# Head rounds of a two-layer transformer block: order of logarithms, weight splits, decay rows and panels

## The chip, the cores and the metric

One core of a Trainium2 chip runs the whole program as one launch. The metric is device time in microseconds (us), median over runs. The engines are TensorE (PE in the profile; its weight loads are PEld), VectorE (DVE), ScalarE (ACT), GpSimd (POOL) and SyncE (SP), which issues most transfers. An engine works through its own instructions in the order in which they are written; between engines the order is set by semaphores.

## The reference, cut to what matters

Two layers over 256 latent and 256 context tokens of width 1024, all float32. Each layer has a feed-forward half, a token mixer and a second feed-forward half. The mixer has three branches (attention, short convolution, gated delta rule); the change is in the third.

```python
DN_HEADS, DN_DIM, CONV_WIDTH = 8, 128, 3
def _dn_inputs(p, dn_conv):
    y = jax.nn.silu(_dwconv(p[6], dn_conv)).astype(jnp.float32)
    q, k, v = [t.reshape(B, T, DN_HEADS, DN_DIM) for t in jnp.split(y, 3, axis=-1)]
    return (_l2norm(q), _l2norm(k), v) + tuple(...)
def _gated_delta_chunked(q, k, v, g, beta, s0):
    gc = jnp.cumsum(chunks(g), axis=-1)
    diff = gc[..., :, None] - gc[..., None, :]
    decay_mat = jnp.where(incl, jnp.exp(jnp.where(incl, diff, 0.0)), 0.0)
    a_mat = jnp.where(strict, jnp.einsum('nbhid,nbhjd->nbhij', kb, kc) * decay_mat, 0.0)
    sol = lax.linalg.triangular_solve(a_mat, rhs, left_side=True, lower=True, unit_diagonal=True)
    attn_intra = jnp.einsum('nbhid,nbhjd->nbhij', qc, kc) * decay_mat
    def step(s, inp): ...   # v_new = u - w s; o = q e^g s + attn_intra v_new; s = s e^g_last + k' v_new
```

It runs in both directions of time for eight heads in each layer. In the last layer only the 256 latent tokens need an output, so queries and output gates are wanted for those alone; keys and values for all 512.

## The kernel before

Every weight matrix comes from HBM as panels of 128x1024 floats. SP loads a panel into `raw`; ACT rounds it to `whi` and DVE subtracts to `wlo` (both called `split`). PE then multiplies 24 times (8 tiles of rows, each `whi` by `uh`, `whi` by `ul`, `wlo` by `uh`), 512 tokens wide or 256. Four panels make a block, and panel j of a block goes to PSUM bank j. SP loads a panel when the `wlo` of the one in its place a block earlier is written; ACT rounds when PE is done with it (`panel_done`).

**A head round.** `heads` on each engine runs the delta rule. One head's four panels (query, key, value, gate) are one block B. Round b works on two heads at once: for head b-1 it solves the triangular system and runs the recurrence, in both directions d = 0 and 1; for head b it makes the inputs. Rounds 1 to 7 of each layer are of this form (`follow`), 14 in all; rounds 1 to 6 are a hardware loop. Round 8 finishes the last head. On PE a round is:

- 14 half levels (`level(v, d)`), in which the inverse of the triangle is doubled. DVE masks one product into `Pm`, ACT copies the other to `QTh`; PE waits for both two half levels later. After each, `project(3)` issues three of the panel multiplications.
- three products that correct the inverse: `lx_sum`, `x2_sum`, `xf_sum`, each followed by `project(3)`. ACT copies the result of the second (L891 in the profile); DVE makes `XTf` from the third (L1668).
- four steps s of the recurrence: `ks_sum`, DVE's `Rr` (L1675), `y_sum`, DVE's `vd`, `ds_sum`, DVE's new state `St` (L1692, L1695), with 15 panel multiplications between them.
- the front of the next head (`output_and_front`): transposes of value and key, the Gram matrix, 27 panel multiplications, and DVE's `Gs`, `AT` (`low_a`), a split and `first_level`.

A round issues 96 panel multiplications: panels 2 and 3 of block B, then 0 and 1 of B+1. Panel 0 of B+1 begins at the third correction, at `project(3)` behind `xf_sum`. It writes bank 0. In the same round bank 0 holds the squared sum of the key, so `project` waits there for `pair_done[0]`, which ACT raises when it has taken the logarithms (`prep_rsqrt`, L785 to L789).

Each half level leaves DVE and ACT room for other work, and their part of `head` puts it at hand-picked places `at` = 2v + d: the convolution of the three inputs (`prep_in`, `prep_tap`, `prep_conv`, `prep_silu`), the splits, and on DVE the decay rows (`decay`): per direction four `scalar_tensor_tensor` of 128x128, `gcr` minus the column `hgc` plus a mask. `gcr` is a row of cumulated gates that a transfer broadcasts (`load_rows`). ACT makes the exponential of a whole row of 512 (`decays`, L806). POOL multiplies `Qt` and `IT` at the head of a round (L489, L493) and subtracts the low half of the output (L495).

Of the kernel before, what the change touches and what calls it, by code (L numbers as in the profile page):

```python
# [134 lines left out]
def build(nc, stream, h_in, vecs_in, rows_in, wab_in, consts_in, cond_in, gcd, out):  # L135
# [7 lines left out]
    with ctx:  # L143
# [329 lines left out]
        def _(pool):  # L473
# [7 lines left out]
            def heads(l):  # L481

                c0 = CTX if l == DEPTH - 1 else 0
                with pool.Fori(0, DNH) as b:
# [9 lines left out]
                    pool.wait_ge(E["bh_ready"], o + 1)  # L494
                    pool.tensor_tensor(bl[:, ds(b, 1), c0:T].rearrange("p a t -> p (a t)"), gate[:, c0:T],  # L495
                                       bh[:, ds(b, 1), c0:T].rearrange("p a t -> p (a t)").bitcast(f32),
                                       ALU.subtract).then_inc(E["head_ready"], 1)
# [11 lines left out]
        def _(act):  # L509
# [219 lines left out]
            def prep_in(l, b, n):  # L729
# [6 lines left out]
                act.activation(pre[:, j, a:2, 1:257], bank[j][:, :].rearrange("p (s t) -> p s t", s=2)[:, a:2, :], ACT.Identity,  # L736
# [43 lines left out]
            def prep_rsqrt(l, b):  # L780
# [8 lines left out]
                act.sem_inc(pair_done[0], 1)  # L789
                for n, a in ((0, 0), (1, c0)):  # L790
                    act.activation(hrs[:, n, a:T], hrs[:, n, a:T], ACT.Exp, scale=-0.5).then_inc(E["l2_rstd"], 1)
# [8 lines left out]
            def decays(l, b):  # L800
# [39 lines left out]
            def head(l, b, follow):  # L840
# [7 lines left out]
                for v in range(7):  # L848
                    for d in range(2):
# [15 lines left out]
                        if at == 4:  # L865
                            split(B, 3)
# [9 lines left out]
                        if at == 8:  # L876
                            split(B + 1, 0)
# [5 lines left out]
                        if at == 11:  # L883
                            split(B + 1, 1)
                        if at == 12:
# [11 lines left out]
                log_exp()  # L897
                if follow:
                    prep_rsqrt(l, b)
                    decays(l, b)  # L900
                    gate_in(l, b)
                output_and_front(l, b, True, follow)

            def heads(l):
# [27 lines left out]
                split(B0 + 1, 2)  # L932
                with steps.loop(1, DNH - 1, 3) as b:
# [255 lines left out]
        def _(dve):  # L1189
# [345 lines left out]

            def prep_conv(l, b, n):
# [27 lines left out]
            def decay(l, b, d):  # L1564

                f = l * DNH + b
                if d == 0:
                    wait(dve, E["dm_ready"], 2 * f)
                    dve.tensor_copy(hgc[:, :], tab[:, ds(b, 1), 8 * HB_GC:8 * HB_GC + 8].rearrange("p a n -> p (a n)")).then_inc(E["hgc_ready"], 1)
                    dve.wait_ge(E["hgc_ready"], f + 1)  # L1570
                    dve.wait_ge(gcr_loaded, 16 * f + 16)
                    wait(dve, E["it_ready"], 2 * f)
                for c in range(TC):
                    last = stt(out=DT[:, d, 128 * c:128 * c + 128], in0=gcr[:, d, 128 * c:128 * c + 128],
                               scalar=hgc[:, 4 * d + c:4 * d + c + 1], in1=cst[:, C_NM + 128 * d:C_NM + 128 * d + 128],
                               op0=ALU.subtract, op1=ALU.add)
                last.then_inc(E["dm_ready"], 1)

            def output_and_front(l, b, output, front):
# [20 lines left out]
                if front:  # L1600
# [4 lines left out]
                    if not output and l == 0:  # L1605
                        decay(l, b, 0)
                    q_norm(l, b)
                    if not output:
                        for d in range(0 if l else 1, 2):
                            decay(l, b, d)  # L1610
                if front:
# [6 lines left out]
                    if output:  # L1618
                        split(P[("head", l)][0] + b + 1, 2)
# [11 lines left out]
            def head(l, b, follow):  # L1631
                B = P[("head", l)][0] + b
                o = l * DNH + b - 1
                if follow:
                    prep_vec(l, b)
                for v in range(1, 7):
# [1173 lines left out]
```

## Time and profile before

| | |
|---|---|
| median of 3 runs | 3138.06 us (3137.23 to 3140.63) |
| profiled execution, its time | 3135.32 us |
| its span, first to last instruction | 3133.5 us |
| TensorE busy | 3026.1 us, 97% of the span |
| mean granted clock of TensorE | 0.992 of full speed |
| follow rounds in layer 0 | about 53.9 or 52.4 us each |
| follow rounds in layer 1 | about 48.9 to 49.8 us each |

A line of the profile names the line of the kernel, engine, operation and tiles (`out<-in`). "Idle before" is how long the engine had nothing to run before that instruction, with what released it. PEclk and granted clock are shares of TensorE's full 2.4 GHz. Rounds are told apart by POOL's instruction L495, one in each.

### The profile page before, as it was taken

To read this page: it belongs to the slowest core of one execution; us is meant where nothing else is said; L and a number is where in the kernel's file an instruction comes from. 1 tells how busy PE (TensorE), PEld (TensorE's weight loads), DVE (VectorE), ACT (ScalarE), POOL (GpSimd) and SP (SyncE) were. 2 spreads that over 40 slices of the span, in tenths; PEclk is the share of its full clock that TensorE was granted. 3 is DMA by queue.
4 is the path that set the end of the run, shared out by engine and by line. 5 is a ranking of instruction groups with operands and counts; after the bars stand their busy time and mean duration, and the time that the engine had idled before them with its cause. 6 is when DMAs were issued, how large, how long until landed. Compare 5 with 4: busy or idle time off the path is not lost.

```text
span 3133.5 us, 49986 instructions
## 1 busy us (share of the span) xinstructions
PE 3026.1 (97%) x17660; PEld 2506.2 (80%) x17660; DVE 2050.5 (65%) x3838; ACT 1408.8 (45%) x2222; POOL 135.9 (4%) x120
## 2 busy tenths in 40 slices
PE   7999999999999999999999999999989999899998
PEld 5888877777787678888888888888777779699887
DVE  4776777777634744445665775757777776766777
ACT  4222365665544642234222342224665566654654
POOL 0000010101000000001000100001000000000000
PEclk9999999999999999999999999999999999999999
DMA  7544421111122022233443533533111114145554
GB/s 272 188 174 174 167 70 47 47 54 47 55 94 74 28 81 95 100 101 103 174 161 136 187 134 136 197 137 127 62 60 51 50 61 142 61 141 175 165 185 153
DMA packets 101843, 365.61 MB, mean 117 GB/s; under 512 B 11216, under 2 KB 12880, under 8 KB 101584
## 3 DMA queue, kind: packets, MB, share of 16 engines
q1 hardware_dynamic: 98384, 353.02, 32.9%
q10 hardware_dynamic: 3328, 10.81, 1.0%
q8 instruction: 86, 1.41, 0.2%
q14 instruction: 45, 0.37, 0.0%
HBM read 362.67 MB, written 1.11 MB: 116 GB/s over the span
## 4 chain that ended last, share of the span: by engine, by line
PE 85%; ACT 6%; DVE 5%; issue 3%; DMA 1%; ACTq 0%; DVEq 0%; SPq 0%; POOLq 0%; POOL 0%
PE bank L2003 65%; PE bank L1982 4%; PE bank L1984 2%; PE bank L2334 1%; PE bank L2274 1%; DVE wlo L1198 1%; ACT whi L519 1%; PE bank L2342 1%; PE bank L2276 1%; PE bank L2540 1%; PE bank L2354 1%; PE bank L2513 1%; PE bank L2352 1%; PE bank L2324 1%; ACT gc_row L1051 1%
## 5 line engine op out<-in xcount | busy, mean ns | idle before, releaser
L2003 PE MATMUL bank<-uh,whi 128*128 128x512 f32 (+1 forms) x2688 | 1019.9, 379 | 36.5 <-ACTq L789 25.3
L519 ACT ACTIVATE whi<-raw 128x1024 fp32r<-128x1024 f32 x520 | 548.3, 1056 | 996.1 <-PE bank L2003 968.7
L2003 PE MATMUL bank<-uh,wlo 128*128 128x512 f32 (+1 forms) x2688 | 977.2, 364 | 0.3 <-DVE scr L1685 0.3
L2003 PE MATMUL bank<-ul,whi 128*128 128x512 f32 (+1 forms) x2688 | 977.4, 364 | 0.0
L1198 DVE TENSOR_TENSOR wlo<-raw,whi 128x1024 fp32r<-128x1024 f32 x520 | 637.1, 1226 | 386.6 <-ACT whi L519 377.6
L2003 PEld LDWEIGHTS bank<-uh,whi 128*128 128x128 f32 x2688 | 510.4, 190 | 132.2 <-issue 50.8
L2003 PEld LDWEIGHTS bank<-uh,wlo 128*128 128x128 f32 x2688 | 509.4, 190 | 78.5 <-issue 6.2
L2003 PEld LDWEIGHTS bank<-ul,whi 128*128 128x128 f32 x2688 | 510.9, 190 | 69.3 <-issue 6.3
L2003 PE MATMUL bank<-bh,whi 128*128 128x512 f32 (+1 forms) x930 | 340.1, 366 | 0.8 <-DVE bl L1920 0.8
L2003 PE MATMUL bank<-bl,whi 128*128 128x512 f32 (+1 forms) x930 | 337.6, 363 | 0.0
L2003 PE MATMUL bank<-bh,wlo 128*128 128x512 f32 (+1 forms) x930 | 337.6, 363 | 0.0
L2003 PEld LDWEIGHTS bank<-bh,whi 128*128 128x128 f32 x930 | 175.4, 189 | 29.3 <-DVE bl L1920 1.0
L2003 PEld LDWEIGHTS bank<-bl,whi 128*128 128x128 f32 x930 | 175.5, 189 | 28.3 <-issue 0.7
L2003 PEld LDWEIGHTS bank<-bh,wlo 128*128 128x128 f32 x930 | 175.5, 189 | 27.3
L1217 DVE SCALAR_TENSOR_TENSOR scr<-ada_raw,gc_row 128x1024 f32<-128x1024 f32 x128 | 156.2, 1220 | 0.0
L1217 DVE SCALAR_TENSOR_TENSOR xtf<-ada_raw,lmat 128x1024 f32<-128x1024 f32 x128 | 155.9, 1218 | 0.0
L1982 PE MATMUL bank<-uh,whi 128*128 128x512 f32 x416 | 144.0, 398 | 1.4 <-DVE uh L1299 0.9
L479 POOL TENSOR_TENSOR scr<-scr 128x512 f32<-128x512 f32 (+1 forms) x36 | 51.6, 1432 | 2159.3 <-ACT scr L556 2159.3
L1640 DVE TENSOR_TENSOR ada_raw<-bank,cst 128x512 f16<-128x512 f32 x192 | 128.1, 686 | 22.3 <-PE bank L2276 21.9
L852 ACT ACTIVATE ada_raw<-bank 128x512 f16<-128x512 f32 x192 | 111.9, 587 | 18.7 <-PE bank L2276 16.9
L1438 DVE TENSOR_TENSOR scr<-scr,bank 128x512 f32<-128x512 f32 x66 | 45.4, 688 | 114.4 <-PE bank L2003 112.6
L2274 PEld LDWEIGHTS bank<-ada_raw 128*128 128x128 f16 x896 | 51.3, 98 | 84.3 <-issue 49.4
(304 smaller groups left out, 3746.4 us busy)
## 6 DMA issues: line engine op xcount, KB each, us to landing
raw<-stream SPq DMA_DIRECT2D x524, 512.0 KB, 3.3
ada_raw<-stream SPq DMA_DIRECT2D x131, 512.0 KB, 4.3
gc_row<-gc_rows ACTq DMA_DIRECT2D x16, 512.0 KB, 3.6
h<-h_in SPq DMA_DIRECT2D x1, 2048.0 KB, 10.3
m<-stream SPq DMA_DIRECT2D x4, 512.0 KB, 12.2
cst<-consts SPq DMA_DIRECT2D x1, 1104.0 KB, 12.6
scr<-stream SPq DMA_DIRECT2D x2, 512.0 KB, 17.1
lmat<-cond ACTq DMA_DIRECT2D x2, 512.0 KB, 4.0
```

The source lines that it names most:

```text
L479: pool.tensor_tensor(nacc[:, c0:T], nacc[:, c0:T], nsq[:, t % 2, c0:T], ALU.add).then_inc(sq_added, 1)
L519: act.activation(whi[:, j, :], raw[:, j, :], ACT.Copy).then_inc(hi_ready, 1)
L852: act.activation(QTh[:, d, :], bank[4 + d][:, :], ACT.Copy).then_inc(E["qtr_ready"], 1)
L1051: act.activation(PT[:, a, :], bank[6 + a][:, :], ACT.Copy).then_inc(A["s_pt"], 1)
L1198: dve.tensor_tensor(wlo[:, j, :], raw[:, j, :], whi[:, j, :].bitcast(f32), ALU.subtract).then_inc(lo_ready, 1)
L1217: last = stt(out=product[k], in0=adaw[:, s, :], scalar=1.0, in1=cond[k], op0=ALU.mult, op1=ALU.mult, accum_out=msum[:, s, k:k + 1])
L1438: dve.tensor_tensor(hbuf[:, k, c0:T], sil[:, k, c0:T], bank[2 * k + 1][:, c0:T], ALU.mult).then_inc(pair_done[k], 1)
L1640: dve.tensor_tensor(c4d(Pm[:, d, :]), c4d(bank[7 - d][:, :]), mask, ALU.mult).then_inc(E["pm_ready"], 1)
L1982: last = mm(bank[j][:, :], whi[:, j, w], x[:, t, :], start=t == 0, stop=t == kts - 1)
L1984: mm(bank[j][:, CTX:T], wlo[:, j, w], x[:, t, CTX:T], start=False, stop=False)
L2003: last = mm(bank[j if to is None else to][:, c0:c1], w(t, a), x[:, t, c0:c1], start=n == 0, stop=n == 3 * kts - 1)
L2274: mm(qt[:, sl(c)], Pm[:, d, sl(c)], x[:, d, sl(c)], start=v == 0 and c == 0, stop=False, skip_group_check=True)
```

## The change

1. **Logarithms first.** ACT's `prep_rsqrt` is cut in two. `log_exp()` (the load of the function table) and the new `prep_log` (two logarithms and `pair_done[0]`) stand ahead of the two copies of `x2_sum`; the exponentials stay behind them.
2. **Splits.** In a follow round all splits are of block B+1. ACT: panel 0 at place 5 (it was 8), panel 1 behind the decays (it was at 11), panels 2 and 3 behind `gate_in` (they were at 12, and at 4 of the next round). DVE: panel 0 at place 7 (was 9), panels 1 and 2 behind the new state of steps 1 and 2 of the recurrence (they were behind the first `XT` and in the front), panel 3 in the front (was at place 6 of the next round). The first head of a layer splits one panel more.
3. **Decay rows.** DVE's `decay` is gone. POOL adds the mask to `gcr` (`masked`, two operations of 128x512) for head b+1; DVE writes the negated column once (`prep_decay`, 128x8); ACT takes the exponential with that column as bias, in four pieces of 128 for each direction.
4. **Key panel first.** The stream holds key, query, value, gate. `prep_in` reads bank n. In layer 1 panel 0 is now 512 tokens wide and panel 1 256; it was the other way.

```diff
+                def masked(f):
+                    pool.wait_ge(gcr_loaded, 16 * f + 16)
+                    wait(pool, E["at_ready"], 2 * f)
+                    wait(pool, E["it_ready"], 2 * f)
+                    for d in range(2):
+                        pool.tensor_tensor(c4d(DT[:, d, :]), c4d(gcr[:, d, :]), bc(cst[:, C_NM + 128 * d:C_NM + 128 * d + 128], TC, 128),
+                                           ALU.add).then_inc(E["dm_ready"], 1)
...
+                    if follow:
+                        masked(o + 1)
+                    tail(b)
...
                 for d in range(2):
                     act.wait_ge(E["dm_ready"], 2 * f + d + 1)
-                    act.activation(DT[:, d, :], DT[:, d, :], ACT.Exp).then_inc(E["dt_ready"], 1)
+                    if d == 0:
+                        act.wait_ge(E["hgc_ready"], f + 1)
+                    for c in range(TC):
+                        s = slice(128 * c, 128 * c + 128)
+                        last = act.activation(DT[:, d, s], DT[:, d, s], ACT.Exp, bias=hgc[:, 4 * d + c:4 * d + c + 1])
+                    last.then_inc(E["dt_ready"], 1)
...
                 if follow:
                     prep_silu(l, b, 2)
+                    log_exp()
+                    prep_log(l, b)
                 for d in range(2):
                     act.wait_ge(E["x2_sum"], 2 * o + d + 1)
                     act.activation(X[:, d, :], bank[7 - d][:, :], ACT.Copy, scale=-1.0).then_inc(E["x2_ready"], 1)
-                if not follow:
+                if follow:
+                    prep_rsqrt(l, b)
+                    decays(l, b)
+                    split(B + 1, 1)
+                    gate_in(l, b)
+                    split(B + 1, 2)
+                    split(B + 1, 3)
...
-                        if at == 6:
-                            split(B, 3)
-                        if follow and at == 8:
-                            decay(l, b, 0)
-                        if at == 9:
+                        if at == 7:
                             split(B + 1, 0)
...
+                        if follow and s:
+                            split(B + 1, s)
...
-                parts = [_panels(wi[:, o:o + 1024]) for o in (ODN, ODN + 1024, ODN + 2048, OG)]
+                parts = [_panels(wi[:, o:o + 1024]) for o in (ODN + 1024, ODN, ODN + 2048, OG)]
```

On ACT, from the end of the half levels to the front, before (L519 is a split, L891 the copies of `x2_sum`, L523 the table, L527 the logarithms, L791 the exponentials of the norm, L806 those of the decays):

```order
L519 ACTIVATE whi<-raw 128x1024
L855 ACTIVATE scr_r<-bank 128x512
L519 ACTIVATE whi<-raw 128x1024
L855 ACTIVATE scr_r<-bank 128x512
L765 ACTIVATE scr<-scr 128x512
L891 ACTIVATE scr_r<-bank 128x512 x2
L523 ACT_TABLE_LOAD
L527 ACTIVATE scr<-bank,eps 128x512 x2
L791 ACTIVATE scr<-scr 128x512 x2
L806 ACTIVATE m<-m 128x512 x2
L808 ACTIVATE gc_row<-gc_row 128x512 x2
L798 ACTIVATE gate_pre<-bank,hv 128x512
```

and now (L542 is the split, L546 the table, L550 the logarithms, L923 the copies, L837 the decays):

```order
L887 ACTIVATE scr_r<-bank 128x512 x2
L788 ACTIVATE scr<-scr 128x512
L546 ACT_TABLE_LOAD
L550 ACTIVATE scr<-bank,eps 128x512 x2
L923 ACTIVATE scr_r<-bank 128x512 x2
L818 ACTIVATE scr<-scr 128x512 x2
L837 ACTIVATE m<-m,hgc 128x128 x8
L840 ACTIVATE gc_row<-gc_row 128x512 x2
L542 ACTIVATE whi<-raw 128x1024
L825 ACTIVATE gate_pre<-bank,hv 128x512
L542 ACTIVATE whi<-raw 128x1024 x2
```

The two splits between the last half levels are gone, the table and the logarithms stand before the copies, and three splits follow in the time of the recurrence.

On DVE, between the new state of one step of the recurrence (L1713) and the `Rr` of the next (L1693), now (L1234 is the split; before, L1675 followed L1695 directly):

```order
L1713 SCALAR_TENSOR_TENSOR scr<-scr,hb,bank 128x128
L1708 REGISTER_ALU
L1713 SCALAR_TENSOR_TENSOR scr<-scr,hb,bank 128x128
L1233 REGISTER_ALU
L1234 TENSOR_TENSOR wlo<-raw,whi 128x1024
L1693 SCALAR_TENSOR_TENSOR scr<-bank,hb,scr 128x128 x2
```

One split stands between them, at steps 1 and 2.

On POOL, in the loop over rounds now (L508 is `Qt`, L512 `IT`, L491 the mask, L498 the low half of the output; before, the last followed `IT`):

```order
L508 TENSOR_TENSOR m<-scr,gc_row 128x512
L512 TENSOR_TENSOR m<-scr,m 128x512 x2
L487 ISA
L321 REGISTER_ALU
L491 TENSOR_TENSOR m<-gc_row,cst 128x512 x2
L498 ISA
L498 TENSOR_TENSOR bl<-scr,bh 128x512
```

Two operations of 128x512 are added to each round.

## Rows read from the trace of the kernel before

**Rows 1.** Waits of TensorE: waiting line, releaser, total us, times, longest.
```profile
PE bank L2003 <- ACTq L789: 25.3, 14, 1.8
...
PE bank L2274 <- ACT ada_raw L852: 7.5, 15, 0.6
PE bank L2274 <- DVE ada_raw L1640: 7.5, 12, 0.8
PE bank L2003 <- DVE wlo L1198: 4.7, 9, 0.9
PE bank L2300 <- DVE scr_r L1656: 2.0, 7, 0.3
```
**Rows 2.** TensorE's timeline, one round of layer 0: start, length, idle before.
```profile
585.09 1.00 PE L2313 MATMUL bank<-scr_r 128*128 128x128 f32 x8
587.90 0.49 PE L2003 MATMUL bank<-uh,whi 128*128 128x512 f32 x1 [1.80 <-ACTq L789]
...
588.69 0.68 PE L2334 MATMUL bank<-scr,xtf 128*128 128x128 f32 x4
```
**Rows 3.** ScalarE's timeline, same round; last row from a round of layer 1.
```profile
580.00 1.05 ACT L519 ACTIVATE whi<-raw 128x1024 fp32r<-128x1024 f32 x1
...
581.42 0.64 ACT L765 ACTIVATE scr<-scr 128x512 f32<-128x512 f32 x1
584.03 1.11 ACT L891 ACTIVATE scr_r<-bank 128x512 fp32r<-128x512 f32 x2 [1.97 <-PE bank L2307]
585.16 1.28 ACT L523 ACT_TABLE_LOAD   x1
586.46 1.27 ACT L527 ACTIVATE scr<-bank,eps 128x512 f32<-128x512 f32 x2
...
2345.80 0.70 ACT L808 ACTIVATE gc_row<-gc_row 128x256 f32<-128x256 f32 x2
```
**Rows 4.** VectorE's timeline, same round of layer 0.
```profile
585.69 1.28 DVE L1668 TENSOR_TENSOR xtf<-scr_r,bank 128x512 f32<-128x512 f32 x2 [1.96 <-PE bank L2313]
```
**Rows 5.** Windows: us, PE, PEld, DVE, ACT, POOL busy, granted clock, DMA.
```profile
561.62:615.47 53.85, 50.79 (x352) 40.38 (x350) 39.54 (x89) 32.06 (x53) 7.16 (x6) 0.97 0.15 49
615.47:667.84 52.37, 49.30 (x352) 38.98 (x350) 39.32 (x89) 32.07 (x53) 7.16 (x6) 1.00 0.15 50
...
590.00:591.00 1.00, 1.00 (x6) 0.97 (x5) 0.57 (x3) 1.00 (x4) 0.00 (x0) 0.50 0.00 0
```
**Rows 6.** VectorE's timeline in the recurrence: layer 0 step 2, layer 1 step 2.
```profile
596.26 0.61 DVE L1675 SCALAR_TENSOR_TENSOR scr<-bank,hb,scr 128x128 f32<-128x128 f32 x2 [0.94 <-PE bank L2324]
...
2546.37 0.61 DVE L1675 SCALAR_TENSOR_TENSOR scr<-bank,hb,scr 128x128 f32<-128x128 f32 x2 [0.58 <-PE bank L2324]
```
**Rows 7.** TensorE's timeline in layer 1, rounds 2 and 7: first L2334, then L2214.
```profile
2344.78 1.05 PE L2334 MATMUL bank<-scr,xtf 128*128 128x128 f32 x4
...
2357.11 0.60 PE L2214 MATMUL bank<-cst,scr 128*128 128x128 f32 x4
...
2540.51 0.61 PE L2334 MATMUL bank<-scr,xtf 128*128 128x128 f32 x4
...
2553.47 0.60 PE L2214 MATMUL bank<-cst,scr 128*128 128x128 f32 x4
```
**Rows 8.** Front of layer 1: VectorE's split and L1623, then TensorE's next half levels.
```profile
2361.91 1.22 DVE L1198 TENSOR_TENSOR wlo<-raw,whi 128x1024 fp32r<-128x1024 f32 x1
...
2364.39 0.48 DVE L1623 SCALAR_TENSOR_TENSOR m<-bank,vec,m 128x256 f32<-128x256 f32 x1
...
2366.54 0.40 PE L2274 MATMUL bank<-ada_raw 128*128 128x128 f16 x4
```
**Rows 9.** VectorE and GpSimd in layer 0: L1550 grouped, one of it, GpSimd beside it.
```profile
L1550 DVE SCALAR_TENSOR_TENSOR kraw<-scr,hv,kraw x16: 751/754/1658, 424.6 to 2518.5; 128x512 f32<-128x512 f32 x16
...
564.73 1.66 DVE L1550 SCALAR_TENSOR_TENSOR kraw<-scr,hv,kraw 128x512 f32<-128x512 f32 x1
...
562.86 2.99 POOL L489 TENSOR_TENSOR m<-scr,gc_row 128x512 f32<-128x512 f32 x2
```

More of the change, by code:

```diff
@@ L483, in heads, with tail, step @@
                 c0 = CTX if l == DEPTH - 1 else 0
-                with pool.Fori(0, DNH) as b:
+                def masked(f):
[5 more added lines that the diff above has]
+                                           ALU.add).then_inc(E["dm_ready"], 1)
+                def tail(b):
+                    o = l * DNH + b
+                    pool.wait_ge(E["bh_ready"], o + 1)
+                    pool.tensor_tensor(bl[:, ds(b, 1), c0:T].rearrange("p a t -> p (a t)"), gate[:, c0:T],
+                                       bh[:, ds(b, 1), c0:T].rearrange("p a t -> p (a t)").bitcast(f32),
+                                       ALU.subtract).then_inc(E["head_ready"], 1)
+                def step(b, follow):
                     o = l * DNH + b
@@ L493, in heads @@
                         pool.tensor_tensor(IT[:, d, c0:T], KQs[:, c0:T], DT[:, d, c0:T], ALU.mult).then_inc(E["it_ready"], 1)
[L494 to L497, printed above, removed]
+                    if follow:
+                        masked(o + 1)
+                    tail(b)
+                masked(l * DNH)
+                with pool.Fori(0, DNH - 1) as b:
+                    step(b, True)
+                step(DNH - 1, False)
             for l in range(DEPTH):
@@ L789, in prep_rsqrt @@
                 act.sem_inc(pair_done[0], 1)
+            def prep_rsqrt(l, b):
+                c0 = CTX if l == DEPTH - 1 else 0
                 for n, a in ((0, 0), (1, c0)):
@@ L882, in head @@
                             prep_silu(l, b, 1)
-                        if at == 11:
+                        if not follow and at == 11:
                             split(B + 1, 1)
-                        if at == 12:
+                        if not follow and at == 12:
                             split(B + 1, 2)
@@ L896, in head @@
                         raw_gates(l)
[L897 to L901, printed above, removed]
+                    log_exp()
                 output_and_front(l, b, True, follow)
@@ L932, in heads @@
                 split(B0 + 1, 2)
+                split(B0 + 1, 3)
                 with steps.loop(1, DNH - 1, 3) as b:
@@ L1534, in prep_vec, with prep_decay @@
                 dve.tensor_copy(hv[:, :], vec[:, ds(v0, HV)]).then_inc(E["hv_ready"], 1)
+            def prep_decay(l, b):
+                f = l * DNH + b
+                wait(dve, E["dt_ready"], 2 * f)
+                dve.tensor_scalar(hgc[:, :], tab[:, ds(b, 1), 8 * HB_GC:8 * HB_GC + 8].rearrange("p a n -> p (a n)"), -1.0, None,
+                                  ALU.mult).then_inc(E["hgc_ready"], 1)
             def prep_conv(l, b, n):
@@ L1562, in q_norm @@
                     op0=ALU.mult, op1=ALU.mult).then_inc(E["qn_ready"], 1)
[L1564 to L1577, printed above, removed]
             def output_and_front(l, b, output, front):
@@ L1618, in output_and_front @@
                     if output:
-                        split(P[("head", l)][0] + b + 1, 2)
+                        split(P[("head", l)][0] + b + 1, 3)
                     first_level(0)
@@ L1656, in head @@
                     dve.tensor_tensor(c4d(XT[:, d, :]), bc(ident, TC, 128), c4d(bank[4 + d][:, :]), ALU.subtract).then_inc(E["xt_ready"], 1)
-                    if d == 0:
+                    if not follow and d == 0:
                         split(B + 1, 1)
-                if follow:
-                    decay(l, b, 1)
                 for d in range(2):
@@ L1721, in heads @@
                 dve.wait_ge(tab_ready, l + 1)
+                prep_decay(l, 0)
                 output_and_front(l, 0, False, True)
                 split(B0 + 1, 2)
+                split(B0 + 1, 3)
                 with steps.loop(1, DNH - 1, HSTEPS) as b:
@@ L2195, in project @@
                             pair_free(G + nxt, j)
-                        all_tokens = nxt == 0 if not follow else j in (1, 2) or (nxt == 1 and isinstance(b, int) and b == DNH - 1)
+                        all_tokens = nxt == 0 if not follow else j in (0, 2) or (nxt == 1 and isinstance(b, int) and b == DNH - 1)
                         panel(B + nxt, j, uh, ul, 0 if all_tokens else c0, lo=at, hi=at + k)
```

17 lines of the change are left out of this document (6 added, 11 removed).

## The prediction

> **What bounds the kernel now.** TensorE is busy 97% of the span (the table), so only its waits, its clock and the few places where it follows another engine can give time. I first read its waits [rows 1]. The largest has one place: 25.3 us in 14 waits of 1.8, one in each follow round, released by ScalarE at L789, the semaphore behind the two logarithms. The next are 7.5 and 7.5 in the half levels, 4.7 for the split, 2.0 for `XT`. Then I read one round of layer 0 on three engines [rows 2 to 4]. TensorE ends the third correction (start 585.09, 1.00 long) at 586.09 and stands until 587.90, because panel 0 of the next block writes the bank with the squared sums. ScalarE shows why: copies of the second correction 584.03 to 585.14, table 585.16 for 1.28, logarithms 586.46 for 1.27, end 587.73. Behind the wait come three panel multiplications, and `y_sum` (L2334) begins at 588.69. VectorE had `XTf` ready long before: 585.69 plus 1.28 is 586.97.
>
> The wait costs more than itself. Two rounds of layer 0 side by side [rows 5]: 53.85 us at a mean granted clock of 0.97, 52.37 at 1.00. In the first the clock stood at 0.50 at 590 to 591, some 2 us behind the wait, which is the 1.2 GHz level; before it TensorE had been idle 1.8 us. So a fall costs 1.48 us. By the same windows it fell in four of the seven follow rounds of layer 0 and in six of seven in layer 1.
>
> **Part 1, logarithms first.** Will ScalarE have them done before the copies are due? Now it ends the last `prep_silu` at 581.42 + 0.64 = 582.06 [rows 3]. Two splits of 1.05 between the last half levels are removed from ahead of it (the order shows it); the copies from PSUM there wait for TensorE, so I count 1.4 of the 2.1: end 580.7. Table and logarithms take 2.55: 583.3, that is 0.7 before the copies start at 584.03. The copies stay where they are, and the bank is free when TensorE comes. What is late next is `XTf`: the three multiplications run from 586.09 to about 586.9, then `y_sum` needs the first half of `XTf` at 586.4 and the second at 587.0. It starts near 586.9 instead of 588.69. I take 1.75 us a round of the 1.80: 14 x 1.75 = **-24.5**. The falls of the clock in layer 0 go with the wait: 4 x 1.48 = **-5.9**. Those of layer 1 are priced below.
>
> Here the Trainium skill speaks against the change. ScalarE: Activation LUTs, "What ACT_TABLE_LOAD costs", gives a table load 1.28 us and a drain of 1.38 more, 2.66 for every switch. By that rule the logarithms would end at 584.7 and the copies be 0.7 us late, +10 us over 14 rounds. The rows show no such drain: the load starts 0.02 us behind the copies and the logarithm 0.02 behind the load [rows 3], so the trace does not agree.
>
> **Part 2, splits.** Layer 0: TensorE waits for a split in 9 places, 4.7 us [rows 1]. The two longest (0.9 and 0.8) are in the first round of each layer, whose split of panel 2 isn't moved; the others are for panel 3 of block B, which now is split half a round ahead: **-3.0**. The price is paid on VectorE in the recurrence. Between the new state and the next `Rr` it idles 0.94 us in layer 0 and, at step 2, 0.58 in layer 1 [rows 6], and a split takes 1.22 [rows 8], next instruction behind 1.2. What exceeds the idle time is on the path, for TensorE's `y_sum` waits for `Rr`. Layer 0: two splits, each 1.2 - 0.94 = 0.26, x 2 x 7 = **+3.6**. Layer 1: 0.62 and 0.26, x 7 = **+6.2**. Below, this could be nothing if `Rr` could start later unseen, but it is followed at once; above, the full 1.2 for each if the idle time was not free. I take the rows. Is the high half there? ScalarE, from the end of the copies (585.14): two exponentials 1.1 (as two copies of 512 columns take 1.11 [rows 3]), eight pieces of 128, two gate rows 1.1, split 1.0. A piece of 128 isn't in the trace; the nearest row is 256 columns, two in 0.70, 0.35 each [rows 3]. So a piece costs between 0.13 (half of it) and 0.35, and I take 0.26, between the two, with some fixed cost: 2.1 for eight. The first high half comes at about 590.4. VectorE asks for it after the state of step 1; in this round `Rr` of step 2 starts at 596.26, so 595.3 less the 3.2 that are saved ahead of it: 592. It fits with 1.6 us to spare.
>
> In layer 1 the half levels wait for ScalarE (L852, 7.5 us in 15 [rows 1]) and VectorE's `XT` (2.0). Both engines lose two splits there, VectorE also the decays. But one ScalarE split moves ahead of the table for `Silu`, where the longest waits are. I take **-2.0** for ScalarE, bounds 0 and -7.5, and **-2.0** for `XT`.
>
> **Part 3, decay rows.** VectorE gets eight instructions less and one short one more; none was waited for, so nothing by itself. POOL works only at the head of a round and has time for two more operations of 1.5 us (two in 2.99 [rows 9]). It starts them when `gcr` has landed, between half levels 7 and 9. There they can hold up VectorE. L1550 takes 0.75 us, but 1.66 where it meets `Qt` of GpSimd [rows 9], and TensorE's waits for L1640 (longest 0.8) stand behind it. The new operations can meet the second convolution or the split at place 7. Nothing to 0.8 a round; most meetings are hidden by the slack of a half level, so 0.2: **+3**. SBUF — State Buffer of the Trainium skill, "Who interferes with whom", calls the shared ports an exclusive lock, so that the later one waits out the whole instruction. That is the upper end, 0.8 to 0.9 a round, and the 1.66 agrees with it.
>
> **Part 4, key panel first.** Layer 0: nothing. In layer 1 rounds 1 to 6 the recurrence gets the wide panel, the front the narrow one. Round 7 of layer 1 is already wide, at full clock: from `y_sum` to the first transpose of the front 2540.51 to 2553.47, 12.96 us, against 12.33 in round 2, narrow and with the fallen clock [rows 7]. So the stretch grows by 0.63 where the fall goes: 6 x 0.63 = **+3.8**. In the front 24 multiplications are narrower, 24 x 0.13 = 3.1 us less for TensorE (three wide ones took 587.90 to 588.69, 0.26 each [rows 2], a narrow one half). But then VectorE is late: its split starts at 2361.91 and L1623, which TensorE's next half level needs, ends at 2364.87; the half level began at 2366.54 [rows 8]. So it can come 1.6 earlier, and VectorE's remaining five instructions and the new `hgc` hold the second level at about 1.05. I take 6 x 1.05 = **-6.3**, bounds 0 and 3.1 each.
>
> **Sum.** -24.5 - 5.9 - 3.0 + 3.6 + 6.2 - 2.0 - 2.0 + 3 + 3.8 - 6.3 = -27.1. Against the profiled execution's 3135.32 that is 3108.2; its median runs 2.7 above it, so against 3138.06 it is **3111 us**.
>
> **The rivals.** *The clock falls elsewhere* (0.17). In layer 1 TensorE would stand about 1.5 us in all at the front, behind the narrow panel, near the 1.8 that made the clock fall. For: six of seven rounds fell there. Against: the 1.5 is in three pieces, and the round at 1.00 [rows 5] holds a wait of 1.8 in one piece without a fall. A fall in six rounds costs 6 x 1.48 = 9: 3120.
>
> *GpSimd's masks hold up VectorE every round* (0.15), for 0.8 instead of 0.2 us: 14 x 0.6 = 8 more, 3119. For: 1.66 against 0.75. Against: a half level later TensorE has caught up.
>
> *The splits cost in full* (0.05): 28 x 1.2 = 34 instead of 10: 3135, no change. For: VectorE feeds every step there. Against: its idle time is released by TensorE.
>
> *The wait only moves* (0.05): with table and logarithms ahead, the copies of the second correction come late. For: nothing else separates them. At the skill's drain 0.7 a round, 3121; without the spare 1.4 us of part 1 the copies are 0.7 late too; at 1.8 the whole gain of part 1 is gone, 3136 or more.
>
> *Slower* (0.05): VectorE stands at the first split in the recurrence for ScalarE's high half. Behind it wait `Rr`, and so `y_sum` and everything. Each us later than the 1.6 spare costs 14 us; from 1.6 + 1.9 = 3.5 us late the kernel is slower than before. At 4.5 late: 3111 + 14 x 2.9 = 3152. Against: eight small exponentials would have to take 0.8 us each, more than one of 512.
>
> My forecast has 0.53.
>
> **How the numbers follow.** A measurement of this kernel tells about 0.2%, 6 us. The forecast and the first two rivals are faster by more, and half of *the wait only moves*: 0.53 + 0.17 + 0.15 + 0.03 = 0.88 and a little of *in full*; 0.89. Slower 0.05, same 0.06. Lower end: masks free (-3), ScalarE's waits gone (-5.5), the front at 1.6 (-3.3), the first heads of the layers earlier without VectorE's decays (-3): 3096, and I say 3095. Upper end: both first rivals in part, 3111 + 15 = 3126.
>
> **What the changed profile would show.** TensorE's wait for the semaphore behind the logarithms gone; ScalarE's copies of the second correction where they were, behind the table; granted clock 1.00 in the rounds of layer 0 and rounds of 50 to 50.6 us; VectorE without idle time between state and `Rr`, and `Rr` 0.3 us late; in layer 1 a wait for L1623's successor at the front and rounds of about 47. Wrong would make it: a clock under 1.00 in layer 1, waits for L1664 (was L1640) above 0.8, VectorE idle ahead of the splits in the recurrence.

## The result and the profile after

| | before | after |
|---|---|---|
| median, same chip (4 runs each) | 3138.5 us | 3099.45 us (3095.61 to 3103.62) |
| ratio, 95% interval | | 0.9879 [0.9865, 0.9893] |
| profiled execution: span, mean granted clock | 3133.5 us, 0.992 | 3097.5 us, 0.998 |

The change makes the kernel faster by 39 us, or 1.2%. 27 were predicted (3111 us). Between the two profiled executions, which the sum was made for, it is 36.0 us. The direction and the main mechanism were as forecast; the time lies in the range of 3095 to 3126 and 12 us below the value.

TensorE's waits after the change (waiting line, releaser, total us, times, longest), the view of [rows 1]:

```profile
PE bank L2296 <- DVE ada_raw L1664: 12.6, 18, 1.1
PE bank L2296 <- DVE m L1646: 7.0, 6, 1.3
PE bank L2296 <- ACT ada_raw L884: 6.2, 16, 0.6
PE bank L2356 <- DVE scr L1693: 4.5, 7, 0.7
PE bank L2025 <- DVE wlo L1234: 2.4, 2, 1.6
```

The wait of 25.3 us behind the logarithms has no successor here. Two waits are new: for L1646 (was L1623) at the front of layer 1, and for L1693, which is `Rr` (was L1675) in the recurrence. The waits for `XT` (L1656) and for VectorE's operand of the second correction behind it (L1663) are gone. The waits for VectorE's half levels (L1664, was L1640) have grown from 7.5 to 12.6.

The third correction and `y_sum` on TensorE's timeline (start, length), the place of [rows 2]:

```profile
579.12 1.00 PE L2335 MATMUL bank<-scr_r 128*128 128x128 f32 x8
579.96 0.44 PE L2025 MATMUL bank<-uh,whi 128*128 128x512 f32 x1
...
580.71 0.83 PE L2356 MATMUL bank<-scr,xtf 128*128 128x128 f32 x4
```

From one start to the other it is 1.59 us; it was 3.60. The panel multiplication follows with no gap. ScalarE's timeline shows why (last column: idle before), the place of [rows 3]:

```profile
574.21 0.62 ACT L788 ACTIVATE scr<-scr 128x512 f32<-128x512 f32 x1
574.85 1.28 ACT L546 ACT_TABLE_LOAD   x1
576.14 1.27 ACT L550 ACTIVATE scr<-bank,eps 128x512 f32<-128x512 f32 x2
578.13 1.09 ACT L923 ACTIVATE scr_r<-bank 128x512 fp32r<-128x512 f32 x2 [0.72 <-PE bank L2329]
...
580.14 2.44 ACT L837 ACTIVATE m<-m,hgc 128x128 f32<-128x128 f32 x8
582.48 1.14 ACT L840 ACTIVATE gc_row<-gc_row 128x512 f32<-128x512 f32 x2
583.52 1.05 ACT L542 ACTIVATE whi<-raw 128x1024 fp32r<-128x1024 f32 x1
```

Table and logarithms end at 577.41, and ScalarE still idles 0.72 us before the copies of the second correction, where the prediction had 0.7. That spare time exists in layer 0 only. In rounds 2 to 6 of layer 1 it is the logarithms that release the copies (L550), though no wait of TensorE follows from it:

```profile
2315.72 1.09 ACT L923 ACTIVATE scr_r<-bank 128x512 fp32r<-128x512 f32 x2 [0.20 <-ACT scr L550]
```

In the round of layer 0 the first high half is written at 584.57, and VectorE begins its low half at 585.98, 1.4 us later (1.6 predicted).

Windows of two rounds (us, then busy time of PE, PEld, DVE, ACT, POOL, the granted clock, DMA): one of layer 0, then one of layer 1, the view of [rows 5]:

```profile
555.85:606.43 50.58, 49.16 (x352) 38.94 (x349) 37.43 (x81) 33.54 (x59) 10.85 (x8) 1.00 0.15 52
...
2295.69:2341.55 45.86, 42.23 (x336) 34.95 (x333) 36.41 (x81) 30.20 (x59) 6.70 (x8) 1.00 0.16 57
```

Rounds of 53.9 or 52.4 us have become 50.6, all alike. In layer 1 rounds of 48.9 to 49.1 have become 45.9, one of them 46.4. The stage of layer 0 up to the end of its heads ends 18.9 us earlier, the rounds of layer 1 take 17.9 us less, and the rest of the program differs by under 2 us.

Cut at TensorE's own instructions, one round of each layer divides as follows (us, before and after; in layer 0 it is a round in which the clock had fallen):

| stretch | layer 0 | layer 1 |
|---|---|---|
| half levels | 20.87, 20.75 | 19.02, 18.65 |
| first to third correction | 4.14, 4.07 | 4.57, 3.75 |
| third correction to `y_sum` | 3.60, 1.59 | 3.73, 1.74 |
| `y_sum` to the front (recurrence) | 14.61, 13.55 | 12.33, 13.28 |
| front | 10.63, 10.62 | 9.43, 8.44 |

### The profile page after: what moved, and what is told of

Same layout as the page of the kernel before. It is cut to its first block, busy times and chain, and to the rows that moved or that the text cites. A ratio compares the mean times of both kernels' runs of the same rounds, so it can differ in the third digit from the quotient of the medians.

```text
span 3097.5 us, 49996 instructions
## 1 busy us (share of the span) xinstructions
PE 3003.2 (97%) x17660; PEld 2488.3 (80%) x17660; DVE 2023.5 (65%) x3710; ACT 1429.8 (46%) x2318; POOL 190.7 (6%) x152
## 4 chain that ended last, share of the span: by engine, by line
PE 83%; DVE 7%; ACT 5%; issue 4%; DMA 1%; SPq 0%; DVEq 0%; ACTq 0%; POOL 0%; POOLq 0%
PE bank L2025 64%; PE bank L2004 4%; DVE wlo L1234 2%; PE bank L2006 2%; PE bank L2356 1%; PE bank L2296 1%; ACT whi L542 1%; PE bank L2322 1%; PE bank L2298 1%; PE bank L2562 1%; PE bank L2390 1%; ACT ada_raw L884 1%; PE bank L2535 1%; ACT gc_row L1087 1%; ACT scr L1115 1%
## 5 line engine op out<-in xcount | busy, mean ns | idle before, releaser
L542 ACT ACTIVATE whi<-raw 128x1024 fp32r<-128x1024 f32 x520 | 546.7, 1057 | 995.7 <-PE bank L2025 967.8
L1234 DVE TENSOR_TENSOR wlo<-raw,whi 128x1024 fp32r<-128x1024 f32 x520 | 637.6, 1227 | 383.6 <-ACT whi L542 376.1
L1664 DVE TENSOR_TENSOR ada_raw<-bank,cst 128x512 f16<-128x512 f32 x192 | 127.4, 686 | 33.2 <-PE bank L2298 32.6
```

The costliest lines, as they stand in the source:

```text
L542: act.activation(whi[:, j, :], raw[:, j, :], ACT.Copy).then_inc(hi_ready, 1)
L1234: dve.tensor_tensor(wlo[:, j, :], raw[:, j, :], whi[:, j, :].bitcast(f32), ALU.subtract).then_inc(lo_ready, 1)
L1664: dve.tensor_tensor(c4d(Pm[:, d, :]), c4d(bank[7 - d][:, :]), mask, ALU.mult).then_inc(E["pm_ready"], 1)
```

## The experiments

Each was timed beside the kernel before (medians of 3136.6 to 3138.6 us). "Changed" is the kernel after the change.

| run | what | median us | ratio to before, interval |
|---|---|---|---|
| e0 | changed, again | 3098.87 | 0.9875 [0.9860, 0.9891] |
| e1 | changed, part 1 undone | 3136.86 | 0.9997 [0.9987, 1.0006] |
| e9 | changed, part 2 undone | 3108.47 | 0.9904 [0.9889, 0.9919] |
| e3 | changed, part 3 undone | 3098.30 | 0.9876 [0.9861, 0.9891] |
| e4 | changed, part 4 undone | 3099.79 | 0.9878 [0.9863, 0.9893] |
| e10 | changed, parts 3 and 4 undone | 3099.15 | 0.9879 [0.9863, 0.9896] |
| e2 | before, part 1 alone | 3107.80 | 0.9903 [0.9888, 0.9918] |
| e7 | before, seven idle multiplications in the gap | 3138.91 | 1.0002 [0.9993, 1.0011] |
| e7b | before, four of them | 3125.12 | 0.9955 [0.9941, 0.9968] |
| e5 | changed, low half of panel 3 a round later | 3111.68 | 0.9914 [0.9900, 0.9928] |
| e6 | e5, and panel 1 out of the recurrence | 3108.12 | 0.9903 [0.9889, 0.9917] |
| e8 | changed, three low halves one place earlier | 3096.61 | 0.9866 [0.9851, 0.9881] |

**Part 1 undone** (e1): the logarithms go back behind the copies.

```diff
                     prep_silu(l, b, 2)
-                    log_exp()
-                    prep_log(l, b)
...
                 if follow:
+                    log_exp()
+                    prep_log(l, b)
                     prep_rsqrt(l, b)
```

> The changed kernel with part 1 alone undone: table and logarithms stand behind the two copies of the second correction again. Theory (the wait for bank 0 and the clock behind it were most of the gain): TensorE's 1.8 us wait is back in 14 rounds, 2.0 us a round to the first y_sum, 28 us, and the clock falls again in some ten rounds at 1.5 us each: 3128 to 3142 us. Rival (the gain comes from the freed half levels, by splits and decay rows, and the wait would have gone with them): 3100 to 3108.

All the gain is gone: what is left is 1.6 us, and the interval holds 1. TensorE's waits show that the old one is back, 1.8 us on average in each of the 14 rounds, and the granted clock is 0.992 again:

```profile
PE bank L2025 <- ACTq L812: 25.6, 14, 1.9
```

Three of the six rounds of layer 0 between marks took 53.9, the others 52.4. Those of layer 1 took 47.6 to 49.8.

**Part 1 alone** (e2): the same lines in the kernel before, with its splits where they were.

```diff
                     prep_silu(l, b, 2)
+                    log_exp()
+                    prep_log(l, b)
```

> The kernel before with part 1 alone: table and logarithms ahead of the copies, splits, decays and panels as before. Theory: ScalarE ends its last silu at 582.06, so table and logarithms end at 584.6 and the copies come 0.6 us late; the wait goes, net 1.4 us a round, 20 us, and 6 us for the clock in layer 0: 3108 to 3116 us. Rival (the moved splits are not needed for it, the late copies are hidden behind the three panel multiplications): 3098 to 3105. Rival (a table load costs about 1.4 us more than its row shows): copies 2 us late, 3130 to 3138.

30.7 of the 39 us, at the lower edge of the theory (3108). Rounds of layer 0 take 50.95, of layer 1 47.0. But now the copies of the second correction are late. ScalarE's timeline has a split between the last half levels and no idle time from there to the copies:

```profile
575.97 1.05 ACT L519 ACTIVATE whi<-raw 128x1024 fp32r<-128x1024 f32 x1
576.91 0.59 ACT L859 ACTIVATE scr_r<-bank 128x512 fp32r<-128x512 f32 x1
577.39 0.64 ACT L765 ACTIVATE scr<-scr 128x512 f32<-128x512 f32 x1
578.04 1.28 ACT L523 ACT_TABLE_LOAD   x1
579.34 1.26 ACT L527 ACTIVATE scr<-bank,eps 128x512 f32<-128x512 f32 x2
580.72 1.08 ACT L897 ACTIVATE scr_r<-bank 128x512 fp32r<-128x512 f32 x2
```

And TensorE waits for them in every round:

```profile
PE bank L2320 <- ACT scr_r L897: 3.1, 14, 0.3
```

The row also decides on the drain. ScalarE: Activation LUTs of the Trainium skill, "What ACT_TABLE_LOAD costs", gives a switch of tables 2.66 us in all. The trace does not agree. Here ScalarE is never idle, and from the start of the load to the first logarithm it is 1.30. With the page's drain of 1.38 more, TensorE would by my estimate wait some 1.6 us at this place instead of 0.2 to 0.3.

**Part 2 undone** (e9): the splits go back to their places, ScalarE's panels 1 and 2 between the last half levels, VectorE's out of the recurrence.

```diff
-                    split(B + 1, 1)
                     gate_in(l, b)
-                    split(B + 1, 2)
-                    split(B + 1, 3)
...
-                        if follow and s:
-                            split(B + 1, s)
```

> The changed kernel with part 2 alone undone: all splits at their old places on both engines. Theory (parts 3 and 4 are worth nothing, as their runs showed, so that the 9 us between the kernel with part 1 alone and the whole change are part 2): 3104 to 3110 us, the corrections' copies 0.3 to 0.6 us late and waits for the split of panel 3 back. Rival (part 2 takes in the recurrence what it gives in the half levels): 3096 to 3102.

Some 9.3 us slower than the changed kernel (9.0 and 9.6 against its two medians), as the theory said. From part 1 alone (e2) to parts 1 and 2 (e10) it is nearly the same, 8.7. The rounds of layer 0 take 50.95 and those of layer 1 46.9, against 50.57 and 45.86. TensorE's waits of this kernel:

```profile
PE bank L2022 <- DVE wlo L1232: 13.9, 16, 1.6
PE bank L2293 <- DVE ada_raw L1662: 11.3, 14, 1.2
...
PE bank L2332 <- ACT scr_r L925: 3.6, 7, 0.6
PE bank L2319 <- DVE scr_r L1676: 2.4, 7, 0.5
```

Beside the changed kernel, 11.5 us more for the low halves, 3.6 for the copies and 2.4 for `XT`; the changed kernel pays 4.5 at `Rr` and, at the half levels, 1.3 more for VectorE and 5.8 more for ScalarE (6.2 against 0.4). These waits do not add up to the 9.3. The stretches do better. Here they are summed over the seven follow rounds of each layer (half levels: rounds 2 to 7), for the kernel before, e9 and the changed kernel:

| stretch | layer 0: before, e9, changed | layer 1: before, e9, changed |
|---|---|---|
| half levels | 125.3, 127.3, 124.5 | 114.1, 116.4, 112.8 |
| first to third correction | 28.9, 28.8, 28.5 | 31.9, 34.8, 26.4 |
| third correction to `y_sum` | 25.7, 12.1, 11.1 | 24.7, 12.2, 12.1 |
| recurrence | 97.3, 93.0, 95.1 | 87.5, 87.7, 93.3 |
| front | 74.4, 74.4, 74.4 | 66.3, 60.1, 60.1 |

From e9 to the changed kernel, part 2 gives 8.4 us in the corrections of layer 1, 6.4 in the half levels and some 1 behind the third correction, and takes 7.7 in the recurrence. The last is seen in a round of layer 1. TensorE's `y_sum` of the four steps and the first transpose of the front, in e9:

```profile
2324.48 0.79 PE L2353 MATMUL bank<-scr,xtf 128*128 128x128 f32 x4
...
2327.39 0.75 PE L2353 MATMUL bank<-scr,xtf 128*128 128x128 f32 x4
...
2330.29 0.75 PE L2353 MATMUL bank<-scr,xtf 128*128 128x128 f32 x4
...
2336.91 0.60 PE L2233 MATMUL bank<-cst,scr 128*128 128x128 f32 x4
```

and steps 1 and 2 in the changed kernel:

```profile
2321.04 0.75 PE L2356 MATMUL bank<-scr,xtf 128*128 128x128 f32 x4
...
2324.65 0.75 PE L2356 MATMUL bank<-scr,xtf 128*128 128x128 f32 x4 [0.68 <-DVE scr L1693]
```

With a split between them, step 2 begins 3.61 us behind step 1; it was 2.90. The whole stretch is 12.43 us in e9 and 13.28 in the changed kernel.

**Parts 3 and 4 undone, one at a time and together** (e3, e4, e10): `decay` on VectorE again with exponentials of whole rows; query first in the stream, so that panel 1 of layer 1 is the wide one.

```diff
-                    if follow:
-                        masked(o + 1)
...
+                        if follow and at == 8:
+                            decay(l, b, 0)
...
-(ODN + 1024, ODN, ODN + 2048, OG)
+(ODN, ODN + 1024, ODN + 2048, OG)
```

> The changed kernel with part 3 undone: the decay rows are made by VectorE as before (at place 8 and behind XT), ScalarE takes one exponential for each direction, GpSimd adds no mask. Theory (VectorE's decay rows were hidden, GpSimd's masks hold it up little): 3096 to 3102 us, the same as the changed kernel. Rival (VectorE's relief gave the 0.8 us a round that the corrections of layer 1 became shorter): 6 to 10 us slower than the changed kernel. Rival (the masks cost 0.8 us a round through the shared port): 8 to 11 us faster than it.

> The changed kernel with part 4 undone: query panel first, so that in layer 1 the recurrence of rounds 1 to 6 has the narrow panel and the front the wide one. Theory: the front takes back 1.0 us a round, the recurrence gives up to 0.9: 3099 to 3105 us. Rival (the recurrence follows VectorE and gives nothing back): 3105 or more. Rival (narrow is as good in the recurrence as in the front and the front's wait for VectorE eats the gain): 3096 to 3099.

> Parts 3 and 4 undone together, so only the logarithms first and the splits are left of the change. Undone one at a time, part 3 gave 3098.30 and part 4 3099.79, against 3099.45 and 3098.87 of the whole change. Theory: parts 1 and 2 carry the whole gain and the other two nothing together either: 3096 to 3102, rounds of layer 0 about 50.6, of layer 1 46.0 to 46.3, granted clock 0.997 or more, no wait behind the logarithms, and no wait for the narrow key panel at the front. Rival: with the panel order of before the second split in the recurrence is paid in full at steps 1 and 2 when VectorE also carries the decay rows, so the two parts were covering for each other: 3104 or more, with TensorE's waits for VectorE's half levels and for the recurrence above 20 us together.

None of the three differs from either median of the changed kernel by more than 1.2 us. What each part does is seen in the waits. Without part 3, VectorE's half levels and ScalarE's:

```profile
PE bank L2294 <- DVE ada_raw L1659: 9.6, 14, 1.0
PE bank L2294 <- ACT ada_raw L867: 9.2, 24, 0.7
```

The masks cost 3.0 us at VectorE (12.6 against 9.6) and ScalarE is waited for 3.0 less (6.2 against 9.2). Without part 4 the front's wait of 7.0 is not there, but `Rr` is waited for longer (7.1 against 4.5), and ScalarE too (7.1 against 6.2):

```profile
PE bank L2296 <- DVE ada_raw L1664: 9.8, 18, 0.8
PE bank L2356 <- DVE scr L1693: 7.1, 13, 0.8
PE bank L2296 <- ACT ada_raw L884: 7.1, 18, 0.7
```

Its rounds of layer 1 take 46.05, against 45.86. Without part 4 the front of a round is 1.0 us longer (9.43 against 8.44). In return the recurrence is 0.2 shorter, and so are, by 0.3 each, the stretch from the third correction to `y_sum` and the half levels. So part 4 mostly moves time, and parts 1 and 2 carry the whole gain.

**The clock by itself** (e7, e7b): the kernel before, with multiplications of constants by constants put into TensorE's gap. Their results go to a bank that nothing reads.

```diff
                     last.then_inc(E["xf_sum"], 1)
+                if follow:
+                    keep_busy(7)
                 project(3)
```

> The kernel before, with seven multiplications of 256 columns (ones by constants, into a bank that is free) behind the third correction of each follow round, where TensorE waits 1.8 us. Their product is used by nothing. The wait stays, but TensorE is not idle. Theory (the wait also costs a fall of the clock, 1.5 us in ten rounds): 3120 to 3128 us, granted clock 0.997 or more. Rival (the rounds with a fall are longer for another reason): 3136 to 3141 at the same clock.

> The kernel before with four multiplications of 256 columns of unused data behind the third correction, instead of seven: by an earlier row three of them take 1.3 us, so four fit into the 1.8 us of the wait where seven (3.0 us) ran over it by 1.2. Theory (each fall of the clock costs 1.5 us, ten rounds): rounds of layer 0 all 52.4 to 52.6 us, 3120 to 3128 us. Rival (the fall costs nothing where the recurrence follows VectorE): 3135 to 3141.

With seven nothing is gained, against the forecast, and the run tells little of what a fall costs: from the first of them to the panel behind them it is 2.9 us, 1.1 more than the gap. Yet the granted clock is 0.998, and every round of layer 0 took about 53.35, which is 52.37 and 1.0 more. With four (`keep_busy(4)`) they end just as the gap does, and the window over this place shows the clock whole, where [rows 5] had 0.50 in it:

```profile
585.00:592.00 7.00, 6.99 (x42) 5.64 (x41) 3.81 (x12) 5.93 (x10) 0.00 (x0) 1.00 0.00 0
```

TensorE starts the panel at 587.30, no later than before in the cycle of the round, and all rounds of layer 0 take 52.35. Those of layer 1 take 48.06, where it was 48.9 to 49.1. The wait is still there, only filled, so the 13.3 us gained (9.6 between the two profiled executions) are the clock's alone: 1.5 us for a fall in layer 0, 0.8 to 1.0 in layer 1. From here to part 1 alone it is another 17.3 us, for the wait itself. The stretches behind the third correction gave 26.7 us, but the corrections, with late copies, took 5.3 of them back, and the recurrence 3.8.

**Repeat** (e0), the changed kernel unedited:

> The changed kernel once more, on the same chip as the next three. Theory: 3096 to 3102 us.

**VectorE's low half of panel 3 out of the front** (e5), to take away the new wait of 7.0:

```diff
-                    if output:
-                        split(P[("head", l)][0] + b + 1, 3)
                     first_level(0)
...
+                        if at == 0:
+                            split(B, 3)
```

> The changed kernel, but VectorE's split of panel 3 moves from the front to place 0 of the next round, behind the first Pm. Theory (in layer 1 TensorE's 1.2 us wait at the front for L1646 stands behind that split): 1.0 us less in six rounds, layer 0 unchanged: 3090 to 3096 us. Rival (the split only moves: the second Pm is late instead and TensorE waits there): 3097 to 3103.

A miss, 13 us slower. Layer 1 gains 0.45 us a round (45.41), but rounds of layer 0 take 53.6 instead of 50.6. At place 0 the split meets GpSimd's operations at the head of the round. VectorE, then GpSimd:

```profile
564.11 2.03 DVE L1234 TENSOR_TENSOR wlo<-raw,whi 128x1024 fp32r<-128x1024 f32 x1
566.06 1.28 DVE L1662 TENSOR_TENSOR ada_raw<-bank,cst 128x512 f16<-128x512 f32 x2
567.26 1.80 DVE L1591 SCALAR_TENSOR_TENSOR kraw<-scr,hv,kraw 128x512 f32<-128x512 f32 x1
569.10 1.65 DVE L1593 SCALAR_TENSOR_TENSOR kraw<-scr,hv,kraw 128x512 f32<-128x512 f32 x1
```

```profile
565.01 3.50 POOL L508 TENSOR_TENSOR m<-scr,gc_row 128x512 f32<-128x512 f32 x2
568.47 3.40 POOL L512 TENSOR_TENSOR m<-scr,m 128x512 f32<-128x512 f32 x2
```

The split takes 2.03 instead of 1.22 and pushes both steps of the first convolution under `Qt` and `IT`: 1.80 and 1.65, where the changed kernel has 0.79 and 1.66. The second convolution meets the masks, 1.68 and 1.66 instead of 0.93 and 0.75. L1662, which reads one input from PSUM, is not slowed: 1.28 us for two, as elsewhere. TensorE pays behind them:

```profile
571.47 0.39 PE L2295 MATMUL bank<-ada_raw 128*128 128x128 f16 x4 [2.02 <-DVE ada_raw L1662]
```

**Panel 1 out of the recurrence as well** (e6), on top of e5:

```diff
-                        if follow and s:
-                            split(B + 1, s)
+                        if follow and s == 2:
+                            split(B + 1, 2)
```

> As the one before, and the split of panel 1 leaves the recurrence: ScalarE makes it between the last two half levels' copies, VectorE behind XT, where it idles 2 us for the first correction. Theory (each split in the recurrence costs what exceeds VectorE's idle time there, 0.3 us in layer 0 and 0.6 in layer 1): another 6 us less, 3084 to 3090 us. Rival (ScalarE's copy of X is late by its split and the corrections wait): no better than the kernel before it, or slower.

A miss too: 3.6 us faster than e5, and the intervals of the two overlap. Yet the split did cost what the theory said: the recurrence of layer 1 is 12.55 us, against 13.27 in e5. Nearly half of this is lost again in the corrections (4.07 against 3.75), where ScalarE's copies come late (1.5 us in 7 waits), as the rival had it.

**Three low halves one place earlier** (e8): panel 1 behind `XT` in the wait for the corrections, panels 2 and 3 behind steps 1 and 2, none in the front.

```diff
                         if follow and s:
-                            split(B + 1, s)
+                            split(B + 1, s + 1)
```

> The changed kernel with VectorE's splits one panel further ahead: panel 1 behind XT in the wait for the first correction (ScalarE's half of it between the last two half levels), panels 2 and 3 behind the states of steps 1 and 2, none in the front. Theory (the front of layer 1 waits for VectorE, whose split there is 1.2 us; the early half levels, where a split met GpSimd and cost 3 us in layer 0, stay untouched): 1.1 us less in six rounds, nothing in layer 0, 3090 to 3095 us. Rival (ScalarE's split before the last half level makes X late): 3097 to 3105.

The fastest kernel of all, but by 2.3 us against e0, which the intervals do not tell apart. It missed the forecast of 3090 to 3095. The front's wait of 7.0 is gone (the front takes 7.69 us, 0.75 less) and its rounds of layer 1 take 45.42. But ScalarE's copies are again just late, and the corrections take 4.07, 0.32 more:

```profile
PE bank L2293 <- DVE ada_raw L1661: 12.3, 18, 1.0
...
PE bank L2332 <- ACT scr_r L923: 1.5, 7, 0.2
```

## Why the prediction was right, and where it was off

**Part 1, right, in part by luck.** It said -24.5 for the gap and -5.9 for the falls of layer 0, 30.4 together; alone it gave 30.7, and without it nothing is left (e2, e1). The two terms were both off, in opposite directions. The falls were worth 13.3, not 5.9, since those of layer 1 belong to them: the sum had them inside the +3.8 of the key panel. The wait gave 17.3 by itself, not 24.5, because the copies were 0.2 to 0.3 us late. The -24.5 needs them on time, and they are so only because part 2 takes ScalarE's splits away. The prediction had counted on that (1.4 of the 2.1 us), so this cover is in its part 1 and in no term of its part 2. With it the stretch from the third correction to `y_sum` shrank by 27.2 us, 2.0 a round in layer 0 where I had 1.75.

**The sum, term by term**, against the table under e9 (before to changed):

| terms | predicted | measured |
|---|---|---|
| wait behind the third correction | -24.5 | -27.2 |
| falls and splits, recurrence of layer 0 | -5.9 + 3.6 = -2.3 | -2.2 |
| splits and wide panel, recurrence of layer 1 | +6.2 + 3.8 = +10.0 | +5.8 |
| corrections | -2.0 | -5.9 |
| half levels (-3.0 - 2.0 + 3) | -2.0 | -2.1 |
| front of layer 1 | -6.3 | -6.2 |

The rows add up to 37.8 us. The rest of the program became 1.8 us longer, which gives the 36.0 of the two profiled executions. Recurrence of layer 1 (4.2), corrections (3.9) and the wait (2.7) make 10.8; less the 1.8, that is the 9 us by which the sum was off.

**The step that failed: the +3.8 for the wide panel.** It is a difference of two rounds, 12.96 in round 7 and 12.33 in round 2 [rows 7]. But e9 has the wide panel in rounds 2 to 6, at the full clock and without the splits, and there the stretch takes 12.42 to 12.46. Over layer 1 it is 87.7 us, where the kernel before had 87.5: with everything but the splits changed, the growth is 0.2, not 3.8. Round 7 takes 13.03 in e9 as well, with the same width and the same 18 panel multiplications, so its extra 0.6 is not the width. It has two waits for VectorE's `vn` at places where rounds 2 to 6 have none; in the kernel before they are:

```profile
2542.50 0.47 PE L2003 MATMUL bank<-uh,wlo 128*128 128x512 f32 x1 [0.34 <-DVE scr L1685]
...
2545.65 0.47 PE L2003 MATMUL bank<-uh,whi 128*128 128x512 f32 x1 [0.34 <-DVE scr L1685]
```

Why only round 7 has them stays open. Round 7 was not a fair stand-in for the others.

**Part 2: the splits in the recurrence right, the corrections far too small.** Its five terms, -3.0 + 3.6 + 6.2 - 2.0 - 2.0, make +2.8, a cost; undoing it costs 9.3 us (e9).
- *Recurrence, +6.2 and +3.6.* Measured 5.6 and 2.1. Holding each split against VectorE's idle time before `Rr` gave 0.62 and 0.26 us a round in layer 1; the steps behind the two splits became 0.71 and 0.12 longer.
- *Corrections of layer 1, -2.0 for `XT`.* From the kernel before to the changed one they became 5.5 us shorter, 0.8 a round. I had counted L1656 (2.0) and passed over L1663 behind it, 1.6 us in 7 waits, three lines further down in the same view. VectorE's split behind the first `XT` held up both; with the splits moved and the decay rows still on VectorE (e10) neither is left.
- *The same stretch without part 2* is 34.8 in e9, 8.4 more than in the changed kernel. The 2.9 that e9 has more than the kernel before go with the late copies, the cover spoken of above.

**Parts 3 and 4, right in sum.** +3 and 3.8 - 6.3 make +0.5; measured 0 (e10). By its pieces it was less right. With the falls of layer 1 (6 x 0.9 = 5.4) taken out of the +3.8, part 4 stood at +2.9, and undoing it showed -1 to 0 (e4), which the noise does not tell from nothing. The waits for VectorE's half levels grew by the 3 us that were forecast for the masks, but ScalarE's fell by as much; the second half was predicted as -2.0 in part 2. The front of layer 1 shrank by 0.99 us a round (1.05 predicted), with the wait where it was said to be:

```profile
2339.83 0.40 PE L2296 MATMUL bank<-ada_raw 128*128 128x128 f16 x4 [1.21 <-DVE m L1646]
```

**The signs.** One of those that were to make the prediction wrong did appear: the longest wait for L1664 is 1.1 us, above 0.8. The masks are not needed for it, since without them (e3) it is still 1.0. The other two did not.

**The rivals.** *The clock falls elsewhere*: it did not; every follow round stood at 1.00, the one with this wait of 1.21 too. *GpSimd's masks*: 3.0 us at VectorE's half levels, not 11, and nothing in the time. *The splits cost in full*: 7.7 us, not 34. *The wait only moves*: the changed kernel has no wait at the copies, but there is no spare time either in layer 1, and without part 2 the wait moves in part (e2, e9). *Slower*: the high half was 1.4 us ahead of its use, and the eight small exponentials took 0.30 each (I had 0.26), far from 0.8.

**Open.** How the 9.3 us of part 2 divide between ScalarE's places and VectorE's was not tried apart. Why some waits of 1.8 us made the clock fall and others did not isn't answered either.

## What to carry to other kernels

When TensorE waits for a semaphore that stands behind a table load, look at what the waiting work truly needs of that engine, and put it ahead of work that is due later. But price it with the engine's other work in place, since a reorder can need a second one as cover (here the reorder gave 30.7 us alone and 39 with parts 2 to 4, while those without it gave 1.6, within the noise). A wait of TensorE is worth more than its length if the clock falls behind it: fill it with a few idle multiplications once, to learn how much of the loss is clock (13 us of 31 here). Before one round stands in for another, compare the waits inside both. And keep operations of VectorE with two SBUF inputs away from those of GpSimd: a free-looking place at the head of a round cost 3 us a round in e5.

## What was not expected of the hardware

- *VectorE beside GpSimd.* The same operation took 1.22 and 2.03 us (split), 0.75 and 1.65 to 1.80 (512 columns), 0.49 and 1.39 (256 columns). GpSimd was slowed too, two operations in 3.40 to 4.16 instead of 2.98. The added time is 0.8 to 1.05, about one half to two thirds of a GpSimd operation, however short VectorE's own. One meeting in layer 1, VectorE and GpSimd:

```profile
2302.71 1.39 DVE L1593 SCALAR_TENSOR_TENSOR scr<-scr,hv 128x256 f32<-128x256 f32 x1
```

```profile
2302.52 2.73 POOL L491 TENSOR_TENSOR m<-gc_row,cst 128x512 f32<-128x512 f32 x2 [2.86 <-DMA gc_row<-gc_rows]
```

- *Filler keeps the clock.* Four multiplications of 256 columns in a gap of 1.8 us removed every fall in the follow rounds (e7b). They work on constants; nothing reads what they write.
- *Table load.* No drain is seen on either side of it, in any of the kernels that were looked at: 1.28 us, with 0.01 to 0.02 before and after.
